# The last mixer's weighted sums of values, as three products of high and low parts

## The chip, the cores and the metric

The kernel runs on one core of one Trainium2 chip. The metric is the device time in microseconds (us) of one execution; lower is better. The engines of the core are TensorE (PE in the profile, its weight loads PEld), VectorE (DVE), ScalarE (ACT), GpSimd (POOL) and SyncE (SP, which here only issues DMAs). They run side by side, each through its own list of instructions in program order, and meet through semaphores.

## The reference, cut to what matters

The kernel computes two transformer blocks for 256 tokens of width 2048 (with 16 extra "meta" tokens in the second). The change lies in the last mixer of the second block, a gated linear attention (GLA) with 4 heads, each with 256 key and 512 value channels, run in both directions:

```python
def gla_chunked(q, k, v, g, strict):              # one direction, chunks of 64 tokens
    b = jnp.cumsum(gc, axis=3)                    # sums of the log decays in a chunk
    q_dec = qc * jnp.exp(b)
    k_inv = kc * jnp.exp(-b)
    k_end = kc * jnp.exp(b_last - b)
    scores = jnp.einsum('bhncd,bhnsd->bhncs', q_dec, k_inv)
    o_intra = jnp.einsum('bhncs,bhnse->bhnce', jnp.where(mask, scores, 0.0), vc)
    ...                                           # a scan over chunks adds what lies further off

def gla_mixer(h, w_in, gk_up, gk_bias, o_norm, w_out):
    ...
    o = (o_f + o_b).transpose(0, 2, 1, 3)[:, pad:]
    o = rmsnorm_2(o, o_norm).reshape(B, L, GLA_VALUE_DIM)
    return (o * jax.nn.silu(g_out[:, pad:])) @ w_out
```

The kernel has no scan over chunks: with decayed keys for near and far chunks it makes the whole table of scores of a head (256 queries by 256 keys, both directions added, and 16 rows for the meta tokens). Then `o` of a head is one weighted sum: values (512 channels) times that table. Inputs and outputs are fp32.

## The kernel before, in words

Nearly all of the time goes to products of activations with weights that come from memory once. A weight unit is a tile of 128x1024 fp32, read by SP into the ring `raw` (8 slots). ACT copies it to a high part in fp32r (a reduced form of fp32 that TensorE takes, L707), DVE subtracts that from the whole and so makes the low part (L1394), both in the ring `wboth` (4 slots, made 3 units ahead). The activations are kept as high and low parts too (`aboth`), and TensorE adds three fp32r products for each tile (`PASSES`: high by high, high by low, low by high; L2317 in `features`). The activations' columns are read there in turns (`in_turns`: 0, 128, 1, 129, ...), and who reads the result takes them apart again (`untwined`, `halves`).

The stages are the list `STREAM`. Those that bear on the change are `gv` (the values of the GLA, 4 trips of 8 units), `gg` (its output gate, 4 trips of 8 units) and `gout` (the output projection). In `gg` a unit is 24 matmuls of 256 columns, and the attention of the four heads is laid between the units: head h begins at unit 8h (`HEAD_AT`), and `head_step(h, lag)` says what each engine does behind the unit that stands `lag` units after it. This order is written out by hand, for each engine apart; only semaphores tie the engines together. The steps that matter:

- lag -6: DVE makes the exponents of the end-decayed keys (`kendf`, `kendb`, L2125 to L2130), ACT their exponentials (L1303) and those of `kinv` (L1307). POOL multiplies the four tiles by the keys as they come (L2960, L2963).
- lag -5: ACT makes the exponentials of `qdec` (L1312) and the decays of whole chunks `dec` (L1313, L1314).
- lag 0 and 1: TensorE makes the near scores (L2826) and the far ones (L2834), DVE masks and gathers them in `sc` (128x512, L2178 to L2188); those of the meta tokens go to `scm` as parts (ACT L1317, L1318, DVE L2191).
- lag 3: TensorE makes `o`, for each of 4 value tiles two products of the fp32 tiles `v3` and `sc` (L2878) and one of the parts for the meta tokens (L2879). ACT squares it (`osq`, L1326).
- between lag 3 and 4: DVE adds the squares (`squares_added`, L2229, L2231), and behind the unit of lag 4 TensorE sums them over the channels with a matrix of ones (L2884). ACT and DVE make the norm's factor from it, scale `o` (L2199) and multiply by the gate (L2222).

As heads are 8 units apart, lag -6 and -5 of head h+1 fall in the same units as lag 2 and 3 of head h.

Of the kernel before, what the change touches and what calls it, by code (L numbers as in the profile page):

```python
# [23 lines left out]
P = 128  # L24
D = 2048
# [104 lines left out]
def two_blocks_kernel(nc, A, out):  # L130

    ctx = ExitStack()
    with ctx:
# [151 lines left out]
        dec = sb("dec", [P, 2, 2, 4], F32, at_=tmp_at + 2 * T2 * 4)  # L285

# [79 lines left out]
        def unit_source(ph, i, j):  # L366
# [22 lines left out]
            if ph == "lr":  # L389
# [26 lines left out]
        v_low, pT_low, scm_low, up_hi, up_lo = map(sem, "v_low pT_low scm_low up_hi up_lo".split())  # L416
# [24 lines left out]
        e_q, e_k, e_d, e_dec, d_sub, q_dec, k_inv, k_end, k_far, sc_sum, x_sum, xm_sum, sc_part, sc_own, sc_ready, scm_ready, \  # L441
            o3_ready, o3_sq, o3_sum, o3_root, o3_rstd, o3_scaled, z3_ready, z3hi = map(
                sem, "e_q e_k e_d e_dec d_sub q_dec k_inv k_end k_far sc_sum x_sum xm_sum sc_part sc_own sc_ready scm_ready "
# [88 lines left out]
        BIAS_AFTER = 20  # L532

# [84 lines left out]
        def _(sp):  # L618
# [67 lines left out]
            sp.wait_ge(e_q, 2 * GL_HEADS)  # L686
            sp.dma_start(xtok[:, :, :].rearrange("p t n -> p (t n)"), park_dram).then_inc(x_back, 16)
# [9 lines left out]
        def _(act):  # L697
# [599 lines left out]
            def head_step(h, lag):  # L1297
# [10 lines left out]
                if lag == -5:  # L1308
# [5 lines left out]
                    act.activation(dec[:, 1, :, :], lb[:, :, 0:TB:GL_CHUNK], ACT.Exp, scale=SC).then_inc(e_dec, 1)  # L1314
                if lag == 1:
                    act.wait_ge(xm_sum, h + 1)
                    act.activation(scm[0:TM, :], bank[0:TM, 6, 0:TB], ACT.Copy)  # L1317
                    act.activation(scm[32:32 + TM, :], bank[0:TM, 6, 0:TB], ACT.Copy).then_inc(scm_ready, 1)  # L1318
# [23 lines left out]

            def gla(i, j):
                if (i, j) == (0, 0):
                    for tt in range(3):
                        values(TRIPS["gv"] - 1, tt)
                for h in reversed(range(GL_HEADS)):
# [35 lines left out]
        def _(dve):  # L1383
# [776 lines left out]
            def head_step(h, lag):  # L2160

                if lag == -6:
                    to_ends(h)
                if lag == -2:
# [17 lines left out]
                if lag == 1:  # L2182
# [7 lines left out]
                    dve.wait_ge(scm_ready, h + 1)  # L2190
                    dve.tensor_tensor(scm[64:64 + TM, :], bank[0:TM, 6, 0:TB], scm[0:TM, :].bitcast(F32), ALU.subtract)\  # L2191
                       .then_inc(scm_low, 1)
# [19 lines left out]

            def gla(i, j):
                if (i, j) == (0, 0):
                    values_low(TRIPS["gv"] - 1)
                for h in reversed(range(GL_HEADS)):
                    head_step(h, 8 * i + j - HEAD_AT[h])
                    if 8 * i + j == GATED_AT[h]:
                        dve.wait_ge(o3_scaled, 4 * h + 4)
                        dve.wait_ge(acc_free, 4 * (C0["gg"] + h + 1))  # L2220
                        z = gg[:, 4 * h:4 * h + 4, :]
                        dve.tensor_tensor(z, osq3[:, :, :], z, ALU.mult).then_inc(z3_ready, 1)  # L2222
# [46 lines left out]
        def _(pe):  # L2269
# [593 lines left out]
            def head_step(h, lag):  # L2863
# [5 lines left out]
                if lag == 3:  # L2869
                    pe.wait_ge(v3_taken, 3 * TRIPS["gv"])  # L2870
                    pe.wait_ge(sc_ready, 3 * h + 3)
                    pe.wait_ge(scm_low, h + 1)
                    pe.wait_ge(v_low, 6 + GL_HEADS)
                    for v in range(4):
                        col = h * GL_V + v * P
                        o = bank[:, 6 + v // 2, (v % 2) * TB:(v % 2 + 1) * TB]
                        for k in range(2):
                            pe.matmul(o, v3[:, k, col:col + P], sc[:, k, :], start=k == 0, stop=False)  # L2878
# [117 lines left out]
```

## Time and profile before

| | us |
|---|---|
| median of 3 runs | 2173.89 |
| the runs | 2173.82, 2177.01, 2173.89 |
| the profiled execution, its own time | 2173.85 |
| its span in the profile | 2172.1 |
| TensorE busy (share of the span) | 2145.8 (99%) |
| DVE, ACT, POOL busy | 1520.8, 1184.2, 220.5 |

The profiled execution is one run of the program; its span is 1.75 us shorter than its device time. Busy shares are means over stages with different limits. A matmul's mean duration counts its way through the array, which the next one overlaps; how far apart matmuls stand is read from the chain of waits, which gives start and length of pieces laid end to end. An fp32 matmul appears as two records, so that the 32 of L2878 are x64 in a count. `v3` is called `v` there.

### The profile page before, as it was taken

How to read it: one execution, taken by the hardware profiler on the slowest of the kernel's cores; microseconds unless marked ns; L12 is line 12 of the kernel's file. 1: busy time of each engine (PE TensorE's matmuls, PEld its weight loads, DVE VectorE, ACT ScalarE, POOL GpSimd, SP SyncE). 2: the span in 40 equal slices, each digit the busy share in tenths (PEclk: the TensorE clock that was granted, in tenths of full speed). 3: DMA queues.
4: the chain of work that ended last, by engine and by line, in shares of the span. 5: the costliest groups of instructions: out<-in, count | busy, mean ns of one | idle time of the engine just before them, and what ended most of it. 6: DMA issues, size and time to landing. Idle time of an engine off the chain costs nothing.

```text
span 2172.1 us, 38987 instructions
## 1 busy us (share of the span) xinstructions
PE 2145.8 (99%) x14559; PEld 1986.3 (91%) x14559; DVE 1520.8 (70%) x2091; ACT 1184.2 (55%) x1781; POOL 220.5 (10%) x146
## 2 busy tenths in 40 slices
PE   9999999999999999999999999999999999999998
PEld 8888899999889999999988889999999999999987
DVE  6676755668578888888855556999777565567755
ACT  5455654545455555555544446555655565676553
POOL 0000000000003223232300000221000000012110
PEclk9999999999999999999999999999999999999999
DMA  8655566657656565666666665566435647555454
GB/s 291 197 156 163 157 202 211 196 170 240 212 162 200 187 215 185 216 193 194 212 202 203 201 202 177 186 192 194 122 119 182 184 140 234 173 158 146 137 201 157
DMA packets 259012, 405.60 MB, mean 187 GB/s; under 512 B 16671, under 2 KB 115868, under 8 KB 257852
## 3 DMA queue, kind: packets, MB, share of 16 engines
q1 hardware_dynamic: 257204, 396.87, 58.6%
q10 hardware_dynamic: 1688, 7.07, 0.9%
q8 instruction: 82, 1.34, 0.3%
q14 instruction: 38, 0.31, 0.0%
HBM read 396.32 MB, written 4.22 MB: 184 GB/s over the span
## 4 chain that ended last, share of the span: by engine, by line
PE 91%; DVE 5%; ACT 3%; issue 1%; DMA 0%; DVEq 0%; ACTq 0%; SPq 0%
PE bank L2317 30%; PE bank L2313 23%; PE bank L2426 14%; PE bank L2310 12%; PE bank L2909 3%; PE bank L2332 2%; DVE wboth L1394 1%; ACT wboth L707 1%; PE bank L2656 1%; PE bank L2878 1%; PE bank L2834 1%; PE bank L2628 1%; DVE xtok L1548 0%; PE bank L2694 0%; PE bank L2361 0%
## 5 line engine op out<-in xcount | busy, mean ns | idle before, releaser
L1394 DVE TENSOR_TENSOR wboth<-raw,wboth 128x1024 fp32r<-128x1024 f32 (+1 forms) x748 | 909.2, 1229 | 514.7 <-ACT wboth L707 511.9
L707 ACT ACTIVATE wboth<-raw 128x1024 fp32r<-128x1024 f32 (+1 forms) x748 | 771.1, 1039 | 609.8 <-PE bank L2313 263.3
L2313 PE MATMUL bank<-aboth,wboth 128*128 128x512 f32 x2496 | 812.8, 382 | 2.3 <-DVE aboth L1613 1.1
L2310 PE MATMUL bank<-aboth,wboth 128*128 128x256 f32 x2496 | 658.8, 274 | 1.0 <-DVE wboth L1394 1.0
L2317 PE MATMUL bank<-aboth,wboth 128*128 128x272 f32 (+1 forms) x5184 | 624.1, 280 | 4.6 <-DVE aboth L1613 3.1
L2317 PEld LDWEIGHTS bank<-aboth,wboth 128*128 128x128 f32 x5184 | 606.1, 190 | 8.6 <-issue 4.0
L2313 PEld LDWEIGHTS bank<-aboth,wboth 128*128 128x128 f32 x2496 | 461.1, 189 | 60.4 <-issue 1.6
L2310 PEld LDWEIGHTS bank<-aboth,wboth 128*128 128x128 f32 x2496 | 478.2, 192 | 12.6 <-issue 2.7
L2426 PE MATMUL bank<-wboth,ghi 128*128 128x512 f32 x704 | 209.8, 379 | 0.9 <-DVE wboth L1394 0.9
L2937 POOL CAST ghi<-pr 128x256 f32 x44 | 84.4, 1918 | 691.1 <-DVE pr L1882 691.1
L2426 PEld LDWEIGHTS bank<-wboth,ghi 128*128 128x128 f32 x704 | 133.1, 189 | 20.2 <-DVE wboth L1394 1.3
L2426 PE MATMUL bank<-wboth,glo 128*128 128x512 f32 x352 | 133.4, 379 | 0.0
L2426 PE MATMUL bank<-wboth,aboth 128*128 128x512 f32 x384 | 83.3, 379 | 0.0
L2426 PEld LDWEIGHTS bank<-wboth,aboth 128*128 128x128 f32 x384 | 72.4, 189 | 10.2
L1070 ACT ACTIVATE cv<-bank,par 128x256 f32<-128x256 f32 x88 | 44.9, 560 | 56.1 <-DVE bank L1861 56.1
L2426 PEld LDWEIGHTS bank<-wboth,glo 128*128 128x128 f32 x352 | 66.5, 189 | 9.4
L1875 DVE SCALAR_TENSOR_TENSOR cv<-bank,par,cv 128x254 f32<-128x254 f32 (+1 forms) x176 | 70.5, 472 | 0.0
L2317 PE MATMUL bank<-yhi,wboth 128*128 128x256 f32 x384 | 64.5, 275 | 0.0
L2909 PE MATMUL bank<-wboth,aboth 128*128 128x512 f32 x288 | 63.1, 379 | 0.4 <-DVE wboth L1394 0.4
L2909 PEld LDWEIGHTS bank<-wboth,aboth 128*128 128x128 f32 x288 | 54.3, 189 | 8.5 <-DVE wboth L1394 0.8
L2317 PEld LDWEIGHTS bank<-yhi,wboth 128*128 128x128 f32 x384 | 58.4, 192 | 0.0
L1849 DVE TENSOR_REDUCE cv<-bank 128x256 f32<-128x512 f32 x88 | 56.4, 682 | 0.0
(373 smaller groups left out, 1870.4 us busy)
## 6 DMA issues: line engine op xcount, KB each, us to landing
raw<-in_w_up SPq DMA_DIRECT2D x176, 512.0 KB, 4.6
raw<-in_w_in SPq DMA_DIRECT2D x156, 512.0 KB, 4.1
raw<-in_attn_w_in SPq DMA_DIRECT2D x96, 512.0 KB, 4.1
raw<-in_gla_w_in SPq DMA_DIRECT2D x96, 512.0 KB, 3.9
raw<-in_w_down SPq DMA_DIRECT2D x80, 512.0 KB, 4.6
raw<-in_w_out SPq DMA_DIRECT2D x32, 512.0 KB, 4.4
raw<-in_attn_w_out SPq DMA_DIRECT2D x32, 512.0 KB, 4.3
raw<-in_gla_w_out SPq DMA_DIRECT2D x32, 512.0 KB, 4.1
```

The lines of the kernel that those rows point to most:

```text
L707: act.activation(whi[:, u % RING, 0:c], raw[:, u % RAW, 0:c], ACT.Copy).then_inc(whi_ready, 1)
L1070: act.activation(cv[:, t, :], bank[:, 4 * chunk + t, TB:2 * TB], ACT.Identity, bias=par[:, bass.ds(i * 4 + (PAR["conv_b"] + r), 1)], scale ...
L1394: dve.tensor_tensor(wlo[:, u % RING, 0:c], raw[:, u % RAW, 0:c], whi[:, u % RING, 0:c].bitcast(F32), ALU.subtract).then_inc(wlo_ready, 1)
L1849: dve.tensor_reduce(halves(cv[:, t, :]), parts_together(bank[:, 4 * chunk + t, :]), AX.X, ALU.add).then_inc(up_scaled, 1)
L1875: dve.scalar_tensor_tensor(cv[:, t, back:TB], bank[:, 4 * chunk + t, TB:2 * TB - back], tap, cv[:, t, back:TB], ALU.mult, ALU.add).then_in ...
L2310: mm = pe.matmul(bank[:, base + t, 0:T], w[1][:, k, col:col + P], in_turns(rhs(0, k0 + k)), start=False, stop=False)
L2313: mm = pe.matmul(bank[:, base + t, 0:2 * T], w[0][:, k, col:col + P], parts_in_turns(both(k0 + k)), start=first, stop=last)
L2317: mm = pe.matmul(bank[:, base + t, 0:T], w[wp][:, k, col:col + P], in_turns(rhs(ap, k0 + k)), start=begins and k == 0 and (wp, ap) == (0, ...
L2332: mm = pe.matmul(bank[:, first_bank + tt, 0:cols[1] - cols[0]], ha((ahi, alo)[ap], k0 + k, tt * P, P), in_turns(w[wp][:, k, cols[0]:cols[1]]),
L2426: mm = pe.matmul(bank[:, row_bank(b, c, tt), :], tokens_of, in_turns(w[wp][:, k, :]), start=begins and k == 0 and (wp, ap) == (0, 0), stop ...
L2909: mm = pe.matmul(bank[:, b, :], gated(ap, k0 + k)[:, tt * P:(tt + 1) * P], in_turns(w[wp][:, k, :]), start=begins and k == 0 and (wp, ap) ...
L2937: pool.tensor_copy(ghi[:, bass.ds(i * 4 + t, 1), :], pr[:, t % 2:t % 2 + 1, :]).then_inc(ffhi_ready, 1)
```

## The change

The values of a head and its scores are each split in a high fp32r part and a rest, and the two fp32 products for each value tile become six fp32r products (three for each half of the keys), all with their columns in turns. The parts are made like those of the weights: ACT copies to fp32r, DVE subtracts. The scores' parts are made at lag 2 (`score_high`, `score_rest`), and `sc_rest` takes the place of `sc`. The values' parts of a head are made in its lag -5, on ACT behind the exponentials (head 0: in its lag 0), in place of decay sums that nothing needs any more (`v3_high` over `cum`) and of the values themselves (`v3_rest` over `v3`). The product with the gate takes the columns apart again. The reload of the parked `x`, which lies over the same memory as `v3_high`, waits for the last head's sums.

```diff
@@ -283,6 +283,11 @@
             ("kinv", [P, 2, 2, TB], F32), ("kendf", [P, 2, T2], F32), ("kendb", [P, 2, TB], F32), ("kfar", [P, 2, 240], F32),
             ("kback", [P, 2, 192], F32), ("sc", [P, 2, TB], F32), ("osq3", [P, 4, TB], F32), ("scm", [P, TB], F32R))
         dec = sb("dec", [P, 2, 2, 4], F32, at_=tmp_at + 2 * T2 * 4)
+        sc_high = sb("sc_high", [P, 2, TB], F32R, at_=tmp_at + 2 * T2 * 4 + 64)
+        v3_high = sb("v3_high", [P, 2, 8 * T2], F32R, at_=cum_at)
+        sc_at = R2 + 4 * (16 * T2 + 3 * D + KD * TB + 2 * P + T2 + 8 * T2 + 8 * TB + 2 * T2 + 2 * TB + 2 * 240 + 2 * 192)
+        sc_rest = sb("sc_rest", [P, 2, TB], F32R, at_=sc_at)
+        v3_rest = sb("v3_rest", [P, 2, D], F32R, at_=R2 + 4 * 16 * T2)
 
         gate_at = R2 + 4 * (16 * T2 + 3 * D + KD * TB + 2 * P + T2 + 2 * 4 * T2)
         lrT = sb("lrT", [P, T2], F32R, at_=gate_at)
...
@@ -530,6 +535,10 @@
             return None
 
         BIAS_AFTER = 20
+
+        def head_values(t, h):
+
+            return t[:, :, 2 * h * T2:2 * h * T2 + GL_V] if t is v3_high else t[:, :, h * GL_V:(h + 1) * GL_V]
 
         def gated(part, k):
 
@@ -684,6 +693,7 @@
             sp.wait_ge(d_sub, 3 * GL_HEADS)
             sp.wait_ge(e_k, 2 * GL_HEADS)
             sp.wait_ge(e_q, 2 * GL_HEADS)
+            sp.wait_ge(o3_ready, GL_HEADS)
             sp.dma_start(xtok[:, :, :].rearrange("p t n -> p (t n)"), park_dram).then_inc(x_back, 16)
             for n, (tt, c0, c1) in enumerate(OUT_PIECES):
                 sp.wait_ge(out_made, n + 1)
@@ -1312,10 +1322,16 @@
                         act.activation(qdec[:, d, :, :], l[:, :, 0:TB], ACT.Exp, scale=SC).then_inc(e_q, 1)
                     act.activation(dec[:, 0, :, :], lf[:, :, GL_CHUNK - 1:TB:GL_CHUNK], ACT.Exp, scale=SC).then_inc(e_dec, 1)
                     act.activation(dec[:, 1, :, :], lb[:, :, 0:TB:GL_CHUNK], ACT.Exp, scale=SC).then_inc(e_dec, 1)
+                if lag == (-5 if h else 0):
+                    act.wait_ge(v3_taken, 3 * h + 3)
+                    act.wait_ge(e_q, 2 * h + 2)
+                    act.wait_ge(e_k, 2 * h + 2)
+                    act.wait_ge(e_dec, 2 * h + 2)
+                    act.activation(head_values(v3_high, h), head_values(v3, h), ACT.Copy).then_inc(high_made, 1)
                 if lag == 1:
                     act.wait_ge(xm_sum, h + 1)
                     act.activation(scm[0:TM, :], bank[0:TM, 6, 0:TB], ACT.Copy)
-                    act.activation(scm[32:32 + TM, :], bank[0:TM, 6, 0:TB], ACT.Copy).then_inc(scm_ready, 1)
+                    act.activation(scm[32:32 + TM, :], bank[0:TM, 6, 0:TB], ACT.Copy).then_inc(high_made, 1)
                 if lag == 3:
                     act.wait_ge(o3_ready, h + 1)
                     if h == GL_HEADS - 1:
@@ -1340,10 +1356,20 @@
             for g in range(TRIPS["gv"]):
                 trip("gv", g, tiles_to(lambda i, chunk, t: vt3[:, i % 2, t, :], T=T2), after=beside_values)
 
+            def score_high(h):
+
+                act.wait_ge(sc_ready, 3 * h + 3)
+                if h:
+                    act.wait_ge(o3_ready, h)
+                act.activation(sc_high[:, :, :], sc[:, :, :], ACT.Copy).then_inc(high_made, 1)
+
             def gla(i, j):
                 if (i, j) == (0, 0):
                     for tt in range(3):
                         values(TRIPS["gv"] - 1, tt)
+                for h in range(GL_HEADS):
+                    if 8 * i + j == HEAD_AT[h] + 2:
+                        score_high(h)
                 for h in reversed(range(GL_HEADS)):
                     head_step(h, 8 * i + j - HEAD_AT[h])
                 if j == 6:
@@ -2161,6 +2187,10 @@
 
                 if lag == -6:
                     to_ends(h)
+                if lag == (-5 if h else 0):
+                    dve.wait_ge(high_made, 3 * h + 1)
+                    dve.tensor_tensor(head_values(v3_rest, h), head_values(v3, h), head_values(v3_high, h).bitcast(F32), ALU.subtract)\
+                       .then_inc(low_made, 1)
                 if lag == -2:
                     for d in range(2):
                         dve.wait_ge(e_q, 2 * h + d + 1)
@@ -2187,9 +2217,9 @@
                                     bank[0:64, 5, TB:TB + P].rearrange("p (t c) -> p t c", t=2)).then_inc(sc_ready, 1)
                     dve.tensor_copy(blocks(flat, 64, P, 0, TB + P, GL_CHUNK),
                                     bank[64:P, 5, TB:TB + P].rearrange("p (t c) -> p t c", t=2)).then_inc(sc_ready, 1)
-                    dve.wait_ge(scm_ready, h + 1)
+                    dve.wait_ge(high_made, 3 * h + 2)
                     dve.tensor_tensor(scm[64:64 + TM, :], bank[0:TM, 6, 0:TB], scm[0:TM, :].bitcast(F32), ALU.subtract)\
-                       .then_inc(scm_low, 1)
+                       .then_inc(low_made, 1)
                 if lag == 4:
                     dve.wait_ge(o3_root, h + 1)
                     dve.reciprocal(rstd[:, 0:TB], msq[:, 0:TB]).then_inc(o3_rstd, 1)
@@ -2210,16 +2240,24 @@
             for g in range(TRIPS["gv"]):
                 trip("gv", g, after=beside_values)
 
+            def score_rest(h):
+
+                dve.wait_ge(high_made, 3 * h + 3)
+                dve.tensor_tensor(sc_rest[:, :, :], sc[:, :, :], sc_high[:, :, :].bitcast(F32), ALU.subtract).then_inc(low_made, 1)
+
             def gla(i, j):
                 if (i, j) == (0, 0):
                     values_low(TRIPS["gv"] - 1)
+                for h in range(GL_HEADS):
+                    if 8 * i + j == HEAD_AT[h] + 2:
+                        score_rest(h)
                 for h in reversed(range(GL_HEADS)):
                     head_step(h, 8 * i + j - HEAD_AT[h])
                     if 8 * i + j == GATED_AT[h]:
                         dve.wait_ge(o3_scaled, 4 * h + 4)
                         dve.wait_ge(acc_free, 4 * (C0["gg"] + h + 1))
-                        z = gg[:, 4 * h:4 * h + 4, :]
-                        dve.tensor_tensor(z, osq3[:, :, :], z, ALU.mult).then_inc(z3_ready, 1)
+                        z = halves_of(gg[:, 4 * h:4 * h + 4, :])
+                        dve.tensor_tensor(z, untwined_of(osq3[:, :, :]), z, ALU.mult).then_inc(z3_ready, 1)
 
             def squares_added(i, j):
 
@@ -2868,15 +2906,17 @@
                     far_scores(h)
                 if lag == 3:
                     pe.wait_ge(v3_taken, 3 * TRIPS["gv"])
-                    pe.wait_ge(sc_ready, 3 * h + 3)
-                    pe.wait_ge(scm_low, h + 1)
+                    pe.wait_ge(low_made, 3 * h + 3)
                     pe.wait_ge(v_low, 6 + GL_HEADS)
                     for v in range(4):
                         col = h * GL_V + v * P
                         o = bank[:, 6 + v // 2, (v % 2) * TB:(v % 2 + 1) * TB]
                         for k in range(2):
-                            pe.matmul(o, v3[:, k, col:col + P], sc[:, k, :], start=k == 0, stop=False)
-                        mm = pe.matmul(o, v3m[0:64 + TM, col:col + P], scm[0:64 + TM, :], start=False, stop=True)
+                            values_of = [head_values(t, h)[:, k, v * P:(v + 1) * P] for t in (v3_high, v3_rest)]
+                            for vp, sp_ in PASSES:
+                                pe.matmul(o, values_of[vp], in_turns((sc_high, sc_rest)[sp_][:, k, :]), start=(k, vp, sp_) == (0, 0, 0),
+                                          stop=False)
+                        mm = pe.matmul(o, v3m[0:64 + TM, col:col + P], in_turns(scm[0:64 + TM, :]), start=False, stop=True)
                     mm.then_inc(o3_ready, 1)
                 if lag == 4:
                     pe.wait_ge(sc_part, 2 * h + 2)
```

How the instructions stand now on the engines around the sums of head 0 and the preparation of head 1; the piece repeats for each next head (from there with a table load ahead of `kendf` on ACT).

ACT before, from the weight unit behind lag 1 of head 1 to the squares of its `o` (`osq_162`); lag -6 and -5 of head 2 lie in it:

```order
L707 ACTIVATE wboth<-raw 128x1024
L1303 ACT_TABLE_LOAD
L1303 ACTIVATE kendf<-kendf 128x544
L1303 ACTIVATE kendb<-kendb 128x512
L1307 ACTIVATE kinv<-cum 128x512 x2
L707 ACTIVATE wboth<-raw 128x1024
L1312 ACTIVATE qdec<-cum 128x512 x2
L1313 ACTIVATE dec<-cum 128x8
L1314 ACTIVATE dec<-cum 128x8
L1326 ACTIVATE osq_162<-bank 128x512 x2
```

and after the change, with `v_high` for `v3_high` and `v_148` for `v3`:

```order
L717 ACTIVATE wboth<-raw 128x1024
L1364 ACTIVATE sc_high<-sc 128x512
L1313 ACT_TABLE_LOAD
L1313 ACTIVATE kendf<-kendf 128x544
L1313 ACTIVATE kendb<-kendb 128x512
L1317 ACTIVATE kinv<-cum 128x512 x2
L717 ACTIVATE wboth<-raw 128x1024
L1322 ACTIVATE qdec<-cum 128x512 x2
L1323 ACTIVATE dec<-cum 128x8
L1324 ACTIVATE dec<-cum 128x8
L1330 ACTIVATE v_high<-v_148 128x2x512
L1342 ACTIVATE osq_162<-bank 128x512 x2
```

Two copies are new: one of the scores ahead of the table load, one of the next head's values between `dec` and the squares.

DVE before, over the same stretch, from the meta tokens' low part of the scores to the two additions of squares:

```order
L2191 TENSOR_TENSOR scm<-bank,scm 16x256
L1394 TENSOR_TENSOR wboth<-raw,wboth 128x1024
L2125 TENSOR_TENSOR kendf<-cum 128x2x256
L2128 TENSOR_TENSOR kendf<-cum 128x2x16
L2130 TENSOR_TENSOR kendb<-cum 128x512
L1394 TENSOR_TENSOR wboth<-raw,wboth 128x1024
L2229 TENSOR_TENSOR osq_162<-osq_162 128x512
L2231 TENSOR_TENSOR osq_162<-osq_162 128x256
```

and after (`v_rest` is `v3_rest`):

```order
L2221 TENSOR_TENSOR scm<-bank,scm 16x256
L1420 TENSOR_TENSOR wboth<-raw,wboth 128x1024
L2246 TENSOR_TENSOR sc_rest<-sc,sc_high 128x512
L2151 TENSOR_TENSOR kendf<-cum 128x2x256
L2154 TENSOR_TENSOR kendf<-cum 128x2x16
L2156 TENSOR_TENSOR kendb<-cum 128x512
L1420 TENSOR_TENSOR wboth<-raw,wboth 128x1024
L2192 TENSOR_TENSOR v_rest<-v_148,v_high 128x2x512
L2267 TENSOR_TENSOR osq_162<-osq_162 128x512
L2269 TENSOR_TENSOR osq_162<-osq_162 128x256
```

A subtraction stands ahead of `kendf`, and another, of 1024 columns, ahead of the additions of squares.

TensorE before, the two units ahead of the sums of head 0 and the first of these:

```order
L2317 MATMUL bank<-aboth,wboth 128x256 x48
L2878 MATMUL bank<-sc,v_148 128x256 x2
L2879 MATMUL bank<-scm,v3m 128x256
L2878 MATMUL bank<-sc,v_148 128x256 x2
L2879 MATMUL bank<-scm,v3m 128x256
```

and after:

```order
L2355 MATMUL bank<-aboth,wboth 128x256 x48
L2917 MATMUL bank<-sc_high,v_high 128x256
L2917 MATMUL bank<-sc_rest,v_high 128x256
L2917 MATMUL bank<-sc_high,v_rest 128x256
L2917 MATMUL bank<-sc_high,v_high 128x256
L2917 MATMUL bank<-sc_rest,v_high 128x256
L2917 MATMUL bank<-sc_high,v_rest 128x256
L2919 MATMUL bank<-scm,v3m 128x256
```

Two fp32 matmuls (four records in the trace) have become six of fp32r; nothing else moved on this engine.

## Rows read from the trace of the kernel before

**Rows 1.** The page: busy us and share of the span by engine.

```profile
PE 2145.8 (99%) x14559; PEld 1986.3 (91%) x14559; DVE 1520.8 (70%) x2091; ACT 1184.2 (55%) x1781; POOL 220.5 (10%) x146
```

**Rows 2.** Waits from 1950 to 2100: engine, line, releaser; us in total, times, longest.

```profile
PE bank L2317 <- DVE wboth L1394: 1.5, 1, 1.5
...
PE bank L2884 <- DVE osq L2231: 0.2, 1, 0.2
```

**Rows 3.** The chain in order of time, head 1: start us, us, what.

```profile
1997.36 5.55 PE bank L2317 x48
2002.91 0.86 PE bank L2878 x4
2003.78 0.12 PE bank L2879
...
2006.85 2.68 PE bank L2317 x24
2009.53 0.44 PE bank L2884 x2
```

**Rows 4.** ACT in time, head 1: start, us, instruction, [idle before].

```profile
1996.93 1.28 ACT L1303 ACT_TABLE_LOAD   x1
2000.84 0.67 ACT L1303 ACTIVATE kendf<-kendf 128x544 f32<-128x544 f32 x1 [2.63 <-DVE kendf L2128]
...
2003.02 1.04 ACT L707 ACTIVATE wboth<-raw 128x1024 fp32r<-128x1024 f32 x1
...
2005.11 0.20 ACT L1314 ACTIVATE dec<-cum 128x8 f32<-128x8 f32 x1
2006.89 1.09 ACT L1326 ACTIVATE osq<-bank 128x512 f32<-128x512 f32 x2 [1.58 <-PE bank L2879]
```

**Rows 5.** DVE in time, head 1, from the scores to the squares.

```profile
1998.11 0.29 DVE L2188 COPY sc<-bank 64x128 f32<-64x128 f32 x1
...
1998.88 1.23 DVE L1394 TENSOR_TENSOR wboth<-raw,wboth 128x1024 fp32r<-128x1024 f32 x1
2000.02 0.68 DVE L2125 TENSOR_TENSOR kendf<-cum 128x512 f32<-128x512 f32 x1
...
2004.09 1.23 DVE L1394 TENSOR_TENSOR wboth<-raw,wboth 128x1024 fp32r<-128x1024 f32 x1 [2.68 <-ACT wboth L707]
2008.01 0.69 DVE L2229 TENSOR_TENSOR osq<-osq 128x512 f32<-128x512 f32 x1 [2.69 <-ACT osq L1326]
2008.73 0.42 DVE L2231 TENSOR_TENSOR osq<-osq 128x256 f32<-128x256 f32 x1
```

**Rows 6.** POOL in time, head 1: its two products for `kinv`.

```profile
2004.13 3.55 POOL L2963 TENSOR_TENSOR kinv<-kinv,gqk 128x512 f32<-128x512 f32 x2
```

**Rows 7.** All runs of two lines: ns min/median/max, first and last start.

```profile
L2963 POOL TENSOR_TENSOR kinv<-kinv,gqk x8: 1277/2301/2335, 1945.7 to 2037.5; 128x512 f32<-128x512 f32 x8
L2096 DVE TENSOR_TENSOR cum<-cum,zabs x4: 1283/1286/2371, 1872.0 to 1946.8; 128x1088 f32<-128x1088 f32 x4
```

**Rows 8.** DVE and POOL in time, 1945 to 1952, where they meet.

```profile
1945.63 1.23 DVE L1394 TENSOR_TENSOR wboth<-raw,wboth 128x1024 fp32r<-128x1024 f32 x1 [7.27 <-ACT wboth L707]
1945.71 4.58 POOL L2963 TENSOR_TENSOR kinv<-kinv,gqk 128x512 f32<-128x512 f32 x2
1946.77 2.37 DVE L2096 TENSOR_TENSOR cum<-cum,zabs 128x1088 f32<-128x1088 f32 x1
1949.07 2.30 DVE L1394 TENSOR_TENSOR wboth<-raw,wboth 128x1024 fp32r<-128x1024 f32 x1
```

**Rows 9.** The chain in order of time, head 3: the sums, the squares, their total.

```profile
2068.97 0.14 PE bank L2879
...
2071.93 0.67 PE bank L2884 x2
```

**Rows 10.** Groups by form, 1850 to 2172: the exponentials' 512 columns on ACT.

```profile
L1307 ACT ACTIVATE kinv<-cum 128x512 f32<-128x512 f32 x8 | 4.5, 614 | 0.0
```

**Rows 11.** SP's issues in time, 1940 to 2172: the reload of the parked x.

```profile
2136.11 0.34 SPq L687 DMA_DIRECT2D xtok<-parked_x  x1
```

More of the change, by code:

```diff
@@ L415, in two_blocks_kernel @@
             sem, "m_root m_mean m_rstd m_scaled m_made m_hi m_ready".split())
-        v_low, pT_low, scm_low, up_hi, up_lo = map(sem, "v_low pT_low scm_low up_hi up_lo".split())
+        v_low, pT_low, low_made, up_hi, up_lo = map(sem, "v_low pT_low low_made up_hi up_lo".split())
         g_tanh = sem("g_tanh")
@@ L440, in two_blocks_kernel @@
             sem, "x_parked x_back up_clear z_sum z_abs z_min z_exp z_ln z_sub cum_ready v3_turned v3_taken".split())
-        e_q, e_k, e_d, e_dec, d_sub, q_dec, k_inv, k_end, k_far, sc_sum, x_sum, xm_sum, sc_part, sc_own, sc_ready, scm_ready, \
+        e_q, e_k, e_d, e_dec, d_sub, q_dec, k_inv, k_end, k_far, sc_sum, x_sum, xm_sum, sc_part, sc_own, sc_ready, high_made, \
             o3_ready, o3_sq, o3_sum, o3_root, o3_rstd, o3_scaled, z3_ready, z3hi = map(
-                sem, "e_q e_k e_d e_dec d_sub q_dec k_inv k_end k_far sc_sum x_sum xm_sum sc_part sc_own sc_ready scm_ready "
+                sem, "e_q e_k e_d e_dec d_sub q_dec k_inv k_end k_far sc_sum x_sum xm_sum sc_part sc_own sc_ready high_made "
                      "o3_ready o3_sq o3_sum o3_root o3_rstd o3_scaled z3_ready z3hi".split())
```

## The prediction

> **What bounds the kernel now.** I read the busy row first: TensorE is busy for 2145.8 of 2172.1 us, no other engine above 70% [rows 1]. So a saving counts only where TensorE does not wait, and I looked next at its waits from 1950 to 2100, where the four heads lie: 1.5 us once for weights, ahead of head 0, and 0.2 on L2884 [rows 2]. The chain in order of time gives the distances of one head [rows 3]: two units (48 matmuls, 5.55), four times two fp32 products and one for the meta tokens (0.86 + 0.12), another unit (2.68), then the total of the squares, L2884. From that I take head 1 as the pattern, with the clock of the trace of before. Last I read ACT, DVE and POOL over the same stretch [rows 4 to 6], since the change hands its work to them just where L2884 is prepared.
>
> **The products on TensorE.** The sums of a head end at 2006.85 and begin at 2002.91: 3.94 us. The new products have the shape and the form of those of a unit: fp32r, 128 rows, 256 columns in turns, each with its own weights. A unit's cost 2.68 / 24 = 0.112 each [rows 3]. Six for each of four tiles and one for the meta tokens are 28, so 3.13 us: 0.81 less per head, 3.2 over four. The nearest other row bounds it: if a product cost as much as half an fp32 one (0.86 / 4 = 0.216 per record), the sums would take 24 x 0.216 + 4 x 0.12 = 5.66, which is 1.72 more than now. I take 0.112, because the row has the same type, shape and turns. The lower end is not below it; TensorE's other 256-column matmuls stand no closer. The Trainium skill (TensorE: Matmul & The Clock Gate, Back-to-back issue gap) gives sustained spacings of about 81 ns at 128 columns and 131 ns at 512. Between them an estimate for 256 is 98 ns, so 28 products in 2.74 us and 0.4 less than by the row. This trace disagrees with the page (0.112), and the row decides.
>
> **The scores' parts, at no cost.** The last copy of the scores ends at 1998.40 [rows 5]. ACT then makes `sc_high`, 512 columns: 0.62 us by L1307 [rows 10], so to 1999.06. DVE reaches `sc_rest` behind its weight unit at 2000.02, and it takes the place of a subtraction of the same 512 columns (0.68, a step of 0.60 to the next). It is ready at 2000.7; TensorE asks at 2002.91. The cover is 2.2 us, and a weight unit more of delay (1.2) would fit in it. What the insertion does cost is order: everything on DVE behind it comes 0.60 later, `kendf` first. ACT waits for `kendf` at 2000.84 [rows 4], now to 2001.44. The table load that stood ahead now comes behind `sc_high`, from 1999.06 to 2000.35, and stays hidden. With ACT's exponentials, POOL's products and both engines' next weight unit move by 0.60 as well. These units are made three ahead, and DVE idles 2.68 ahead of that unit [rows 5], so TensorE does not wait for weights.
>
> **The values' parts, which decide.** ACT ends `dec` at 2005.31 before, so at 2005.91 now [rows 4]. Then it copies the next head's values, 1024 columns: 1.04 by its weight unit, so from 2005.95 to 2007.0. TensorE ends its sums at 2006.85 - 0.81 = 2006.04, and the squares (1.09), queued behind the copy, now begin at 2006.95 instead of 2006.08 and end at 2008.05. Alone that would still do. But DVE must subtract 1024 columns (1.23, a step of 1.14) ahead of the two additions of squares, and it can begin only when the copy is there, at 2007.04.
>
> Here POOL comes in. Its first `kinv` product starts 0.04 behind DVE's weight unit and takes 2.3 instead of 1.28 [rows 6, 7]; the second takes 1.28. Around 1946 the same pair meets DVE in a row [rows 8]: L1394 undisturbed, `kinv` behind it 2.3, L2096 2.37 where its median is 1.29 [rows 7], a further `kinv` 2.3, L1394 2.30 instead of 1.23. So a POOL product and a DVE operation with both inputs in SBUF run one after the other, whole instruction by whole instruction, in turns. The Trainium skill (SBUF — State Buffer, Who interferes with whom) has this as a lock that the first to start holds, and counts `tensor_tensor` with two SBUF inputs among those that need it. It speaks against this change, and the trace agrees (2.37 against 1.29).
>
> Before, POOL was done at 2007.68 and the additions began at 2008.01: no meeting. Now all is 0.60 later: DVE's weight unit from 2004.69, POOL's first product to 2007.05, its second due at 2007.01, the subtraction at 2007.04. Whichever goes first, two more of about 1.2 follow each other: both done by 2009.4. If the subtraction wins, the waiting product goes ahead of the first addition, as at 1949, and the additions start at the same time. They take 1.15 from the first's start to the second's end [rows 5], so 2010.5, and TensorE starts 0.14 behind [rows 9]: 2010.6. It arrives at 2009.53 - 0.81 = 2008.7. So it waits 1.9 for each of heads 0, 1 and 2, in whose units the next head is prepared. For head 3 there is no next head; its L2884 follows its sums by 2.8 before and after, with the same 0.2 of waiting, and the 0.81 is kept.
>
> Behind L2884 nothing else is late: ACT's further steps are 1 us later, as TensorE is. Head 0's own values' parts go in its lag 0: one subtraction of 1.14 on DVE there delays a weight unit that is made three units, some 8 us, ahead of its use; I put this at 0, at most 0.5.
>
> **Small things.** The gate's product reads its input with a stride; 1.22 now, at most doubled, on heads 0 to 2 in idle time, on head 3 ahead of `gout`, where it could cost up to 1.2; I take 0, since reads in turns from PSUM cost nothing extra. SP's new wait is reached only at 2136 [rows 11], long after head 3's sums at 2069 [rows 9].
>
> **The sum.** Products -0.81 x 4 = -3.2; waits +1.9 x 3 = +5.7; the rest 0: +2.5 on the profiled execution's 2173.85 (its span 2172.1 and 1.75 around it), so 2176.3. The median of the runs shown is 2173.89, the same. By the skill's spacing the three waits would grow by what the sums shrink, and only head 3 would gain 0.4 more: 2175.9.
>
> **Rivals.** (a) *POOL keeps out of the way*: the second `kinv` product comes behind the additions. The subtraction then ends at 2008.3, the additions at 2009.35, TensorE starts at 2009.5 as before. Heads 0 to 2 give nothing, head 3 0.81, together -0.9: 2172.9. For it: the order of two starts 0.03 apart. Against: a waiting product went next each time. (b) *All hidden*: the waits stay at 0.2 in all, -3.2: 2170.6. For it: DVE idles 2.69 ahead of the additions before [rows 5]. Against: that time lies ahead of the copy's end, where the subtraction can't use it. (c) *The products are slower than a unit's*, the other side: at 0.216 the sums take 1.72 more, TensorE reaches L2884 at 2011.2, behind the additions, so no waits but +1.72 x 4 = +6.9: 2180.7. It decides for slower from 0.16 a product on. For it: v_high and v_rest lie apart in memory and the weights change with each product; against: both hold for a unit too. (d) *The chain of the additions is longer*, by a third product of POOL or a slow strided copy: beyond 2.6 us of waiting per head, over 2178.2.
>
> **How the numbers follow.** My forecast has 0.61, (a) 0.13, (b) 0.12, (c) 0.06, (d) 0.05, and 0.03 is left for a gain that I don't see. The forecast's own range is 2174.6 to 2177.8 (waits of 1.4 to 2.4). The range for 8 in 10 takes in (a) and the lower part of (d): 2172.0 to 2178.8. A measurement of this kernel tells a change from none beyond about 0.2%, 4.3 us. Only (c) and (d) pass that upward, so slower 0.10; faster 0.03; within it 0.87.
>
> **What would show it.** Right: the sums of a head from 3.94 to about 3.1; PE L2884 waiting for DVE's L2269 three times near 1.9; the subtraction or a `kinv` product of twice its length in each of three heads; head 3 without that. Wrong: a subtraction of values that ends before 2008.5 on this clock (a); a wait on L2884 below 0.5 (b); sums above 4 us (c); a wait of TensorE for the parts themselves or for `wboth` inside `gg`, which I exclude.

## The result, and the profile after

| | before | after |
|---|---|---|
| median of nine runs each, us | 2175.64 (2173.82 to 2177.01) | 2182.53 (2180.81 to 2184.74) |
| ratio after / before, 95% interval | | 1.0033 (1.0025 to 1.0042) |
| profiled execution, us | 2173.85 | 2182.53 |
| its span, us | 2172.1 | 2180.7 |
| mean granted clock | 0.999 | 0.996 |

The changed kernel is slower by 6.9 us (medians), or 8.6 us between the spans of the two profiled executions. The forecast was +2.5, and 2182.5 lies outside its range. The profiled execution of before is one of its quickest runs, so the two differences are not the same number. The accounting below goes by the spans.

The change inserts lines, so L2884 is now L2924, L2878 is L2917, L2317 is L2355, L2229 and L2231 are L2267 and L2269, L1394 is L1420, and L2963 is L3003.

Busy time of each engine after, from the page, answering [rows 1]:

```profile
PE 2148.1 (99%) x14591; PEld 1989.4 (91%) x14591; DVE 1531.3 (70%) x2099; ACT 1192.3 (55%) x1789; POOL 221.0 (10%) x146
```

TensorE is busy 2.3 us longer, though 3.2 us of products were taken from it. Its waits from 1950 to 2100 (engine, line, releaser, us in total, times, longest), answering [rows 2]:

```profile
PE bank L2924 <- DVE osq L2269: 5.7, 3, 1.9
PE bank L2355 <- DVE wboth L1420: 1.5, 1, 1.5
```

Three waits of 1.9 stand on the total of the squares, as forecast; that is 5.5 more than the 0.2 of before. Now head 1 as the chain of waits shows it in order of time (start, us, what), answering [rows 3]:

```profile
2008.87 0.11 ACT dec L1324
2009.09 1.07 ACT v_high L1330
2010.18 2.26 DVE v_rest L2192
2012.44 0.61 DVE osq L2267
2013.08 0.44 DVE osq L2269
2013.52 0.14 issue
2013.65 0.67 PE bank L2924 x2
2014.32 12.35 PE bank L2355 x96
```

The chain leaves TensorE: it goes through ACT's copy of the values, DVE's subtraction at twice its length, and the two additions. Then come two numbers that nothing in the prediction stands for. The product of L2924 (one fp32 product, which the trace shows as two records) takes 0.67, not 0.44 [rows 3], and the 96 matmuls of the next four units take 12.35 us. The change does not touch these units: before, one of 24 took 2.68 [rows 3], so four take 10.7. The windows show what is different (us, busy time of PE, PEld, DVE, ACT and POOL with counts, granted clock, DMA share, GB/s). After, behind the first, second and third wait:

```profile
1979.60:1984.00 4.40, 4.39 (x24) 4.35 (x25) 4.38 (x5) 1.42 (x2) 0.00 (x0) 0.65 0.38 113
1984.00:1988.00 4.00, 4.00 (x37) 4.00 (x37) 3.44 (x7) 3.20 (x4) 0.00 (x0) 0.96 0.51 138
...
2013.65:2017.65 4.00, 4.00 (x23) 3.95 (x24) 3.98 (x4) 1.42 (x2) 0.00 (x0) 0.67 0.37 103
2047.70:2051.70 4.00, 3.99 (x23) 3.95 (x24) 3.98 (x4) 1.42 (x2) 0.00 (x0) 0.68 0.35 93
```

Before, at the place of the first:

```profile
1978.40:1982.40 4.00, 4.00 (x37) 3.95 (x36) 3.05 (x3) 3.02 (x4) 0.00 (x0) 1.00 0.14 20
```

TensorE starts 23 or 24 matmuls in a window in which it started 37 before. It is busy all the time; each matmul is longer. The granted clock is 0.65 to 0.68 on the mean of these windows, where it was 1.00: for part of them it was at 1.2 GHz, the lower of its two levels. One stretch of the new line shows it too (ns min/median/max); the first row is after, from 1980.3 to 1984.5, the second before at the same place:

```profile
L2355 PE MATMUL bank<-aboth,wboth x25: 275/421/460, 1979.9 to 1984.4; 128*128 128x256 f32 x25
```

```profile
L2317 PE MATMUL bank<-aboth,wboth x93: 275/275/460, 1978.5 to 1989.0; 128*128 128x256 f32 x93
```

DVE and POOL of after in time, where they meet (start, us, instruction, [idle before]), answering [rows 5] and [rows 6]:

```profile
2003.07 0.68 DVE L2246 TENSOR_TENSOR sc_rest<-sc,sc_high 128x512 fp32r<-128x512 f32 x1
...
2007.76 1.23 DVE L1420 TENSOR_TENSOR wboth<-raw,wboth 128x1024 fp32r<-128x1024 f32 x1 [2.70 <-ACT wboth L717]
2010.18 2.26 DVE L2192 TENSOR_TENSOR v_rest<-v,v_high 128x1024 fp32r<-128x1024 f32 x1 [1.20 <-ACT v_high L1330]
2012.37 0.68 DVE L2267 TENSOR_TENSOR osq<-osq 128x512 f32<-128x512 f32 x1
```

```profile
2007.78 3.58 POOL L3003 TENSOR_TENSOR kinv<-kinv,gqk 128x512 f32<-128x512 f32 x2
```

POOL's two products end at 2011.36, and the subtraction, begun at 2010.18 behind ACT's copy, is held until then. That is the meeting that the prediction worked out.

**The account of one head** (0, 1 or 2): sums -0.81; wait +1.89; the start behind it 0.67 - 0.44 = +0.23; four units, in part at the lower clock, 12.35 - 10.72 = +1.63. Together +2.94. Three such heads give +8.8. Head 3 has only the -0.81. The last POOL and DVE work ahead of `gout` adds 0.3: L2949 begins 19.79 us behind L2924 and began 19.47 behind it. The rest, some 0.3, is spread out. The sum is 8.6.

The 0.3 comes from the gate's product, which now reads with a stride. It takes 1.34 where it took 1.22, and 1.55 on head 3. There POOL's three products that begin beside it (L2970) last 8.50 in all, against 8.19 before, and DVE's two subtractions of weight units, which fall beside these, last 5.28 instead of 4.96. In e6 below, whose gate product is the plain one, they last 4.96 again and L2949's counterpart begins 19.48 behind. The product after, then the two subtractions after and before:

```profile
L2260 DVE TENSOR_TENSOR gg<-osq,gg x4: 1336/1342/1554, 1990.7 to 2089.3; 128x1024 f32<-128x1024 f32 x4
```

```profile
2094.50 5.28 DVE wboth L1420 x2
```

```profile
2086.40 4.96 DVE wboth L1394 x2
```

### The profile page after: what moved, and what is told of

The parts are those of the page before. It is cut to its first block, busy times and chain, and to the rows that moved or that the text cites. A ratio compares the mean times of both kernels' runs of the same rounds, so it can differ in the third digit from the quotient of the medians.

```text
span 2180.7 us, 39075 instructions
## 1 busy us (share of the span) xinstructions
PE 2148.1 (99%) x14591; PEld 1989.4 (91%) x14591; DVE 1531.3 (70%) x2099; ACT 1192.3 (55%) x1789; POOL 221.0 (10%) x146
## 3 DMA queue, kind: packets, MB, share of 16 engines
q8 instruction: 82, 1.34, 0.3%
## 4 chain that ended last, share of the span: by engine, by line
PE 89%; DVE 6%; ACT 3%; issue 1%; DMA 0%; DVEq 0%; ACTq 0%; SPq 0%
PE bank L2355 29%; PE bank L2351 23%; PE bank L2464 14%; PE bank L2348 12%; PE bank L2949 3%; PE bank L2370 2%; DVE wboth L1420 1%; ACT wboth L717 1%; PE bank L2694 1%; PE bank L2872 1%; PE bank L2666 1%; DVE xtok L1574 0%; PE bank L2732 0%; PE bank L2399 0%; DMA xtok<-in_x 0%
## 5 line engine op out<-in xcount | busy, mean ns | idle before, releaser
L1420 DVE TENSOR_TENSOR wboth<-raw,wboth 128x1024 fp32r<-128x1024 f32 (+1 forms) x748 | 909.9, 1230 | 511.8 <-ACT wboth L717 508.7
L2355 PE MATMUL bank<-aboth,wboth 128*128 128x272 f32 (+1 forms) x5184 | 629.0, 281 | 4.6 <-DVE aboth L1639 3.1
L2355 PEld LDWEIGHTS bank<-aboth,wboth 128*128 128x128 f32 x5184 | 610.9, 191 | 8.5 <-issue 4.0
L2355 PE MATMUL bank<-yhi,wboth 128*128 128x256 f32 x384 | 64.5, 275 | 0.0
L2949 PE MATMUL bank<-wboth,aboth 128*128 128x512 f32 x288 | 63.3, 380 | 0.5 <-DVE wboth L1420 0.5
L2949 PEld LDWEIGHTS bank<-wboth,aboth 128*128 128x128 f32 x288 | 54.3, 189 | 8.9 <-DVE wboth L1420 1.3
L2355 PEld LDWEIGHTS bank<-yhi,wboth 128*128 128x128 f32 x384 | 58.4, 192 | 0.0
```

The source lines that it names most:

```text
L1420: dve.tensor_tensor(wlo[:, u % RING, 0:c], raw[:, u % RAW, 0:c], whi[:, u % RING, 0:c].bitcast(F32), ALU.subtract).then_inc(wlo_ready, 1)
L2355: mm = pe.matmul(bank[:, base + t, 0:T], w[wp][:, k, col:col + P], in_turns(rhs(ap, k0 + k)), start=begins and k == 0 and (wp, ap) == (0, ...
L2949: mm = pe.matmul(bank[:, b, :], gated(ap, k0 + k)[:, tt * P:(tt + 1) * P], in_turns(w[wp][:, k, :]), start=begins and k == 0 and (wp, ap) ...
```

## The experiments

Two questions were open: whether the wait causes the slow units (the rivals: the sums in their new form, or the operands and DMAs beside the units), and why waits stay when the values' parts are moved. All times are medians; each difference is against the kernel before, run on the same chip beside it (2174.84 for the first four, 2174.0 for the next four, 2174.16 for the last three).

### e1: the values' parts in the next head's own lag 0

```
-                if lag == (-5 if h else 0):      # in ACT's and in DVE's step
+                if lag == 0:
```

> The values' parts of every head are made in its own lag 0 instead of lag -5 (head 0 has them there already); nothing else changes. Theory W (the three waits of TensorE on L2924, 1.9 us each, and the lower clock behind each, 1.9 us each, are the whole loss; both come from the copy and the subtraction standing ahead of the squares): waits on L2924 back to about 0.2 in all, clock 1.00 throughout, sums 3.13 per head, so 3.2 us below the kernel before: about 2172.4 against its 2175.6, ratio 0.9985. Rival S (the parts cost wherever they stand, since DVE and ACT are full in gg): waits appear elsewhere, on wboth or on the parts, and the time stays above the kernel before.

Measured: 2175.14, ratio 1.0000 (0.9991 to 1.0009). The units take 10.72 again and the clock is 1.00, but the 3.2 us did not appear. Three waits of 0.7 remain (2.2 more of waiting than before), with 0.23 at the start behind each and the 0.3 ahead of `gout`: together 3.2. Waits on the total, then the first addition and POOL of head 1:

```profile
PE bank L2924 <- DVE osq L2269: 2.4, 4, 0.7
```

```profile
2007.21 1.66 DVE L2267 TENSOR_TENSOR osq<-osq 128x512 f32<-128x512 f32 x1 [1.27 <-ACT osq L1342]
```

```profile
2004.76 3.56 POOL L3003 TENSOR_TENSOR kinv<-kinv,gqk 128x512 f32<-128x512 f32 x2
```

The addition takes 1.66 instead of 0.69 [rows 5]. It is asked for at 2007.21 and POOL holds it until 2008.32. Before, it came at 2008.01, behind POOL's end at 2007.68 [rows 5, 6]. The sums are 0.8 shorter, so the squares come sooner and run into POOL's second product.

### e2: POOL's products behind the additions

```
                 # POOL, ahead of the two products for kinv
+                if h:
+                    pool.wait_ge(o3_added, 2 * h)
```

> As the changed kernel, but POOL's two kinv products of heads 1 to 3 wait for the additions of squares of the head before, so that they can't stand between DVE's subtraction and these. Theory W with the lock as its part: the subtraction takes 1.23 instead of 2.25, the wait on L2924 falls from 1.9 to about 0.8 per head. If the clock falls behind any wait of this place, the loss behind it stays (1.9 per head) and the time is about 2179; if it needs the longer wait, the loss goes too and the time is near -3.2 + 2.4 = 0.8 below the kernel before, 2174.8. Rival (the subtraction is long by its strided operands, not by POOL): it stays at 2.25 and the time at 2182.

Measured: 2175.45, ratio 1.0003 (0.9994 to 1.0012). All four subtractions are now undisturbed, and three waits of up to 0.9 are left, with the units at 10.72:

```profile
L2192 DVE TENSOR_TENSOR v_rest<-v,v_high x4: 1224/1224/1225, 1962.4 to 2038.7; 128x1024 fp32r<-128x1024 f32 x4
```

```profile
PE bank L2924 <- DVE osq L2269: 2.5, 3, 0.9
```

So the meeting of the two engines is worth 1 us of each wait. The 0.9 that remain are the copy on ACT and the subtraction itself, in turn ahead of the additions.

### e3: TensorE kept busy while it waits

```
                 # PE, at lag 4 of heads 0 to 2, ahead of the wait for the additions
+                for _ in range(8 if h < GL_HEADS - 1 else 0):
+                    pe.matmul(bank[:, 4, TB:TB + P], ones[:, :], ones[:, :], start=True, stop=True)
```

> As the changed kernel, but TensorE runs 8 fp32 matmuls of 128 columns on a matrix of ones (some 1.7 us) into an unused part of bank 4 where it would wait for the additions, for heads 0 to 2. Theory W: TensorE starts L2924 as late as before, but the granted clock behind it stays at 1.00, so four units take 10.7 instead of 12.35: 5.6 us less than the changed kernel, about 2177, which is the sum of the prediction. Rival C (the 12.35 come from something else, slower operands or DVE and ACT behind their time): four units stay at 12.35 and the time at 2182 or above.

Measured: 2179.12, ratio 1.0019 (1.0010 to 1.0028); span 2175.8, 4.9 less than after's. The chain, and the window behind it:

```profile
2010.17 1.79 PE bank L2924 x16
2011.95 0.69 PE bank L2926 x2
2012.64 10.72 PE bank L2355 x96
```

```profile
1980.30:1984.30 4.00, 4.00 (x38) 4.00 (x38) 4.00 (x5) 2.63 (x4) 0.00 (x0) 1.00 0.45 129
```

In this kernel L2924 is the line of the useless products (eight, in 16 records), and the total of the squares is L2926. The squares are as late as in the changed kernel, the sums and units are the same, and TensorE has useless products in place of idling. The clock stays at 1.00, and 3 x 1.63 = 4.9 us come back, the whole difference of the spans. The 5.6 that were expected counted the 0.23 of each start too, which stays (0.69). This is what shows that idling, not the operands or the new sums, made the units slow.

### e4: the values' parts one unit later

```
-                if lag == (-5 if h else 0):
+                if lag == (-4 if h else 0):
```

> As the changed kernel, but the values' parts of heads 1 to 3 are made one step later, in lag -4: on ACT behind the squares of the head before and its next weight unit, on DVE behind the additions of squares. Theory W: the waits on L2924 are gone and it is as fast as the kernel with the parts in lag 0, about 2172.4, since DVE's run from there to the next scores ends with over 3 us idle. Rival S: DVE is full in these units, so a subtraction of 1.2 there makes TensorE wait for weights or for the next scores, 1 us or more per head.

Measured: 2175.54, ratio 1.0001 (0.9992 to 1.0010). Waits of up to 0.8, again from a first addition of 1.66:

```profile
2008.77 1.66 DVE L2267 TENSOR_TENSOR osq<-osq 128x512 f32<-128x512 f32 x1 [1.27 <-ACT osq L1342]
```

### e5: e1 and e2 together

> Values' parts in lag 0 for all heads, and POOL's kinv products of heads 1 to 3 behind the additions of squares. Theory L (with the parts out of the way, what is left of the waits on L2924 is POOL's second kinv product holding up the first addition: it took 1.66 instead of 0.68, and TensorE waited 0.7): the first addition takes 0.7, the wait on L2924 is at most 0.2 in all, and the whole saving of the products is kept, -3.2: about 2171.7, ratio 0.9985. Rival (the additions are late by their own length once the sums are 0.8 shorter): waits of 0.5 and more stay and the time is that of the kernel before.

Measured: 2171.43 (2171.14 to 2172.88), ratio 0.9988 (0.9979 to 0.9997). The best version, 2.6 us below the kernel before. One wait of 0.2 is left, and POOL follows the squares:

```profile
PE bank L2924 <- DVE osq L2269: 0.2, 1, 0.2
```

```profile
2006.70 0.69 DVE L2267 TENSOR_TENSOR osq<-osq 128x512 f32<-128x512 f32 x1 [1.00 <-ACT osq L1342]
```

```profile
2007.93 3.60 POOL L3005 TENSOR_TENSOR kinv<-kinv,gqk 128x512 f32<-128x512 f32 x2 [3.37 <-DVE osq L2269]
```

The 3.2 us of the products are real; 0.2 of them goes at head 1 (its distance to the next is 30.55, the others' 30.31, before's 31.13) and 0.3 at the end.

### e6: the parts made, but the fp32 products kept

```
-    dve.tensor_tensor(head_values(v3_rest, h), ...)     # sc_rest likewise
+    dve.tensor_tensor(head_values(v3_high, h), ...)
...
+    pe.matmul(o, v3[:, k, col:col + P], sc[:, k, :], start=k == 0, stop=False)
```

Differences and copies are made at the same places and not used; the gate's product is the plain one.

> The changed kernel with its parts made as they are, at the same places, but the two fp32 products per tile as before (the parts are written and used by nobody). Theory W: L2884's work starts as late behind the scores as in the changed kernel, TensorE comes 0.8 later, so it waits 1.1 per head for heads 0 to 2: 3.3 above the kernel before if the clock holds behind a wait of 1.1, 8.2 above if it falls there (1.6 over the four units behind each). Rival (the loss hangs on the new products): within 1 of the kernel before.

Measured: 2178.32, ratio 1.0019 (1.0010 to 1.0029).

```profile
PE bank L2921 <- DVE osq L2269: 3.3, 4, 1.1
```

TensorE arrives 0.8 later, so the waits are up to 1.1, and the units of this stretch stay at 10.72. The preparation alone costs 4.3 us: 3.1 of waiting, 0.7 of starts, and 0.5 that these do not account for.

### e7 and e8: the kernel before with a wait put in

```
                 # DVE, ahead of the two additions of heads 0 to 2; e7: (128, 64), e8: (128, 128)
+                if h:
+                    dve.wait_ge(o3_scaled, 4 * h)
+                for n, c in enumerate((128, 64) if h < GL_HEADS - 1 else ()):
+                    dve.reciprocal(rstd[:, 0:c], ones[:, 0:c]).then_inc(g_tanh, 1)
+                    dve.wait_ge(g_tanh, 16 + 2 * h + n + 1)
```

> The kernel before, with two more reciprocals on DVE (128 and 64 columns of ones) ahead of the additions of squares for heads 0 to 2. TensorE waits some 1.2 on L2884 for each. Theory W: +3.6 to +4.3 if the clock holds, 4.9 more if it falls behind waits of this length.

> As the run before, with reciprocals of 128 and 128 columns: TensorE waits some 1.7 on L2884 for heads 0 to 2. Theory W (the clock falls by a wait of this length alone, whatever the products are): three drops of the granted clock, four units behind L2884 take 12.3 instead of 10.7, +5.1 +0.7 +4.9 = +10.7. Rival C (the drop needs the fp32r products of the sums, or the work of the parts): clock 1.00 and +5.8 at most.

Measured: e7 2178.88, ratio 1.0022 (1.0012 to 1.0031), e8 2180.36, ratio 1.0028 (1.0016 to 1.0040). Waits of e7, then of e8:

```profile
PE bank L2889 <- DVE osq L2236: 4.2, 4, 1.4
```

```profile
PE bank L2889 <- DVE osq L2236: 5.4, 4, 1.8
```

In both, all units behind these waits take 10.72. A wait of 1.8 did not bring the clock down here, which the theory had expected of e8. The price of such a wait is still more than its length: e7 waits 4.0 more than before and loses 4.9, and the 0.23 at each start behind a wait gives 0.7 of the difference.

### e9 to e11: longer waits, and the same in e5's kernel

e9 is e8's edit with (128, 128, 48); e10 is the same in e5's kernel; e11 is (128, 128) in e5's kernel.

> The kernel before with reciprocals of 128, 128 and 48 columns ahead of the additions for heads 0 to 2, so that TensorE waits some 2.2 on L2884 (it held the clock at 1.7). Theory T (the length of the wait alone decides, somewhere between 1.74, which held, and 1.89, which fell in the changed kernel): the clock falls behind all three, four units take 12.3, +6.6 +0.7 +4.9 = +12.2 on the kernel before. Theory F (it needs the sums as fp32r products, ahead of the wait, too): the clock holds, +7.3.

> The kernel with values' parts in lag 0 and POOL held (2171.4), with the same three reciprocals: the same wait of 2.2 behind fp32r sums. Both theories: the clock falls three times, +7.3 +4.9 = +12.2 on 2171.4. If it holds here, the drop hangs on something else in the changed kernel.

> As the run before, with reciprocals of 128 and 128 columns: a wait of some 1.7 behind fp32r sums, the length that held behind fp32 sums. Theory T: the clock holds, +5.8 on 2171.4. Theory F: it falls in this run too, +10.7.

| | longest wait | median, us | ratio (95%) | four units behind the three waits |
|---|---|---|---|---|
| e9 | 2.2 | 2183.08 | 1.0042 (1.0027 to 1.0056) | 10.72, 11.75, 10.72 |
| e10 | 2.2 | 2183.16 | 1.0038 (1.0025 to 1.0051) | 10.72, 12.34, 12.21 |
| e11 | 1.7 | 2177.40 | 1.0014 (1.0005 to 1.0024) | 10.72, 10.72, 10.72 |

The chain of e9, then of e10, in order of time:

```profile
1981.40 10.72 PE bank L2322 x96
...
2014.32 1.19 PE bank L2889 x2
2015.51 11.75 PE bank L2322 x96
...
2050.12 10.72 PE bank L2322 x96
```

```profile
1982.10 10.72 PE bank L2360 x96
...
2014.87 12.34 PE bank L2360 x96
...
2049.40 12.21 PE bank L2360 x96
```

Of equal waits of 2.2 in one kernel, one brings the clock down and the next does not. Where it fell, the loss is much the same: 1.03 in the units and 0.52 in the product ahead of them (1.19 instead of 0.67) in e9, 1.62 and 1.49 + 0.14 in e10. At 1.7, e5's kernel with its new sums keeps the clock behind these waits, as the kernel before does in e8. It loses 6.0 us on e5: 5.2 of waiting and 0.5 of starts (one of e5's own starts was already 0.67).

**The same fall where nothing was edited.** The lower clock also appears outside the stretch of the four heads. At 1760 us every kernel of this case has TensorE wait 0.7 us, run eight products of 128 columns, wait 1.1 and go on with a unit. That unit in the kernel before, then in e8, with a window of e8 (granted clock 0.50):

```profile
1762.51 2.92 PE L2317 MATMUL bank<-aboth,wboth 128*128 128x256 f32 x24 [1.10 <-DVE aboth L1613]
```

```profile
1762.48 4.54 PE L2322 MATMUL bank<-aboth,wboth 128*128 128x256 f32 x24 [1.10 <-DVE aboth L1613]
```

```profile
1763.00:1764.00 1.00, 1.00 (x7) 1.00 (x7) 0.51 (x2) 1.00 (x3) 0.00 (x0) 0.50 0.00 0
```

The clock fell there in the traces of e6, e8 and e11, and stayed at 1.00 in the ten others. At 622 us, behind waits of 0.65 and 1.1, it fell in e4 and e10 and in no other. The instructions and the waits at these two places are the same in all thirteen traces, so the kernel's own order does not decide it alone. The times of the kernel before go the same way: of its 78 runs beside the experiments, the 43 with a mean granted clock of 0.999 took 2174.1 on average, the 34 with 0.998 took 2175.3. Two medians may therefore differ by over 1 us by such falls alone, though only some of these runs have a trace. The quickest runs are a second comparison, and they agree with the medians: e5 2171.14 against 2173.82, e6 2177.94 against 2173.82, and e1 2173.94, e4 2174.09 and e2 2174.36 against 2173.90.

## Why the prediction was wrong

**Sums 3.94 to 3.13.** Right. Each of the four tiles takes 0.67 and the meta tokens' product 0.11 behind it, 28 products at 0.112. Rival (c) is out.

**The scores' parts at no cost.** Right: no wait on them appears, and `sc_rest` takes 0.68.

**The values' parts and POOL's turn: waits of 1.9 for heads 0 to 2, none for head 3.** Right in place, mechanism and size (1.9, three times; a subtraction of 2.25; e2 takes 1 us of each wait away by moving POOL alone). Rival (d) is out as written: no wait passed 2.6. Its price came by another way.

**"Waits +1.9 x 3 = +5.7".** This is the step that failed. I priced a wait at its length and took all that TensorE does behind it at the clock of the trace of before, which I had named as my pattern. The wait was followed by four units of 12.35 instead of 10.72, and by 0.23 more for the product of L2924: 1.86 per wait, 5.6 us in all. Added to the forecast of +2.5, that is +8.1 of the 8.6 measured. In the profile before I could have seen that the clock stood at 1.00 from 1950 to 2100 and asked what would hold it there once TensorE idled. It had idled 1.5 us there once [rows 2] and the clock held, which made the omission easy. That each of the three waits would be followed by a fall could not be read from that trace: in e9 and e10 a longer wait was not always followed by one.

**The rest at 0.** Nearly right: the gate's product, put at 0, costs 0.3 ahead of `gout`, by way of POOL.

**Rivals (a) and (b).** Neither occurred, and their times were wrong too. (a) had the waits right: with POOL out of the way, e2 has TensorE waiting up to 0.9 for heads 0 to 2, as (a)'s start at 2009.5 behind an arrival at 2008.7 says. But the span was 0.4 above before's and not 0.9 below it, since the 0.23 of each start and the 0.3 ahead of `gout` stand in no sum of mine. (b) took the squares as ready in time once the values' parts were hidden. e1 and e4 moved the parts away, and waits of 0.7 and 0.8 stayed: the 0.33 between POOL's end and the first addition [rows 5, 6] was smaller than the 0.81 by which the squares moved forward. I had looked at that meeting only with the additions moved back.

**Two bounds of the rivals.** (c) was said to decide for slower from 0.16 us a product on. By my own sum the waits are gone once the sums of a head take 1.07 more, and 4.3 us in all are reached there, which is 0.19 a product. In (d) the same 4.3 us are reached at 2.5 us of waiting, not 2.6. Neither bears on the forecast.

**What stays open.** On the total of the squares, three waits of 1.9 of three were followed by the lower clock in the changed kernel's trace, waits of 2.2 in one case of three (e9) and two of three (e10), and none of 1.8 or less. Length is not the rule, though: at 622 and 1762 us a wait of 0.7 and one of 1.1, close together, were followed by it in five of 26 cases. What decides was not found. It may be chance in the changed kernel too: seven of its nine runs took 2182.2 to 2184.7 at a granted clock of 0.996, the two others 2180.8 and 2181.0 at 0.998 and 0.997, which would fit one fall fewer; no trace of these shows it. The granted clocks of e10's runs, 0.996 to 0.998 against 0.998 and 0.999 in e9, say nothing of the denser sums, as e10's trace has a third fall at 622.

## What to carry to other kernels

Where TensorE is 99% busy, work taken from it is a gain only if whatever it waits for next is earlier by as much: measure the slack of that chain first, against the new arrival and not the old, including VectorE's and GpSimd's meetings on SBUF. Keep preparation for a later stage out of the chain that answers TensorE, even when the engines look idle there; here moving one copy and one subtraction and holding one engine back turned +6.9 us into -2.6. Price a wait of TensorE of about 2 us at up to twice its length, because of what the clock may do to the work behind it. Before a difference of 1 or 2 us is put down to an edit, look in both traces for falls of the clock in places that the edit does not touch.

## What was not expected of the hardware

- The granted clock fell behind waits of TensorE of 1.9 and 2.2 us, to 0.65 to 0.68 on the mean of the 4 us behind it in the changed kernel, and each fall cost 1.55 to 1.63 us of the product and the four units behind the wait. On the same line it did not fall behind the waits of 0.7 to 1.8 in e1, e2, e4, e6, e7, e8 and e11. Eight useless products of 128 columns in the wait held it (e3).
- The same fall came behind waits of 0.7 and 1.1 close together, at 1762 us in e6, e8 and e11 and at 622 us in e4 and e10, and not in the other traces, with the same instructions there (at 1762, 24 matmuls in 4.54 us instead of 2.92).
- The product of L2924 takes 0.67 us behind a wait, without one 0.44, also where the clock stays at 1.00 (e7, e8, e11). A wait of 0.2 is enough (head 3). At head 1 of e5 and in e3, where the matmul lists no wait but its weight load waits 0.2, it takes 0.67 and 0.69 too. Before, [rows 9] had it at head 3, behind a wait of 0.2, and I did not read it so.
- A product on VectorE that reads one SBUF input with a stride takes 1.34 us for 1024 columns, where the plain one took 1.22.
- Either engine can be the one that is held in SBUF. POOL's second product goes first if it is queued first, and it lengthened a 0.69 us addition to 1.66, a 1.22 us subtraction to 2.25. The Trainium skill (SBUF — State Buffer, Who interferes with whom) has the rule that the one that starts first keeps the other out for its whole instruction. The traces agree, and e2 and e5 show that the order of two instructions decides who pays.
